# Attention probabilities turned by DMA instead of by TensorE, with scores three heads ahead

## The reference

```python
mod = jax.nn.silu(c) @ w_ada + b_ada
shift, scale, gate = jnp.split(mod, 3, axis=-1)
h = rms_norm(x, g_norm) * (1 + scale) + shift
q_lat, kv_lat, k_rope, z_a, q_b, k_b, v_b, z_b = split(h @ w_in)
# group A: latent attention, 8 heads of 96 (64 + 32 rotary), values of 64
qa = rotate_tail(rms_norm(q_lat, g_qa) @ w_uq);  ka, va = from(rms_norm(kv_lat, g_kva) @ w_ukv, k_rope)
ya = softmax(qa @ ka.T * MLA_SCALE) @ va * silu(z_a)
# group B: 8 query heads of 64 on 2 key heads, norms and 2-D rotary on q and k
yb = softmax(qb @ kb.T * GQA_SCALE) @ vb * silu(z_b)
x = x + gate * (concat(ya, yb) @ w_out)
```

## Time and profile before

| what | value |
|---|---|
| median of 3 runs | 2575.91 us (2571.5 to 2578.02) |
| span of the profiled execution | 2575.7 us |
| its own time, span and what lies around it | not listed apart; the span is within 0.3 us of the median |
| instructions | 44323 |
| TensorE matmuls, weight loads | 16106 each |
| data moved by DMA | 129.42 MB, 50 GB/s over the span |

### The profile page before, as it was taken

One profiled execution on the slowest core, in us unless ns is written; L12 is line 12 of the kernel. 1 busy time (PEld: TensorE's weight loads), 2 busy tenths in 40 slices (PEclk: granted clock), 3 DMA queues, 4 the chain that ended last, 5 costly groups with the idle time before them and its releaser, 6 DMA issues.

```text
span 2575.7 us, 44323 instructions
## 1 busy us (share of the span) xinstructions
PE 2396.8 (93%) x16106; PEld 1409.9 (55%) x16106; DVE 1343.9 (52%) x2390; ACT 974.0 (38%) x2202; POOL 789.5 (31%) x1325
## 2 busy tenths in 40 slices
PE   6689999899999999999989899979899999999997
PEld 1344554455566566666555455545556656656654
DVE  0444444375656565555545444537555556555563
ACT  0223333133444444444422333422344444444442
POOL 0454321274421231232116632237442123123210
PEclk9799999899999999999999999999999999999999
DMA  7621112121000000000242000023000000000001
GB/s 237 222 96 58 54 52 85 58 94 38 9 9 25 16 24 8 24 17 0 73 155 98 9 17 25 33 101 122 9 9 10 33 24 16 24 33 25 0 25 41
DMA packets 63228, 129.42 MB, mean 50 GB/s; under 512 B 6687, under 2 KB 31365, under 8 KB 63125
## 3 DMA queue, kind: packets, MB, share of 16 engines
q1 hardware_dynamic: 63128, 128.09, 14.3%
HBM read 115.44 MB, written 12.63 MB: 50 GB/s over the span
## 4 chain that ended last, share of the span: by engine, by line
PE 75%; DVE 15%; issue 5%; ACT 2%; POOL 1%; DMA 1%; DVEq 0%; SPq 0%; POOLq 0%; ACTq 0%
PE psum L577 58%; PE psum L567 10%; PE psum L770 6%; DVE region L1019 3%; DVE nmax L1002 3%; DVE hT L882 3%; ACT region L1171 1%; DVE region L977 1%; DVE region L1028 0%; DVE region L979 0%; POOL region L1225 0%; PE psum L571 0%; ACT region L1147 0%; DVE KTa L944 0%; DMA Wq<-in_w_ada 0%
## 5 line engine op out<-in xcount | busy, mean ns | idle before, releaser
L1171 ACT ACTIVATE region<-psum 128x512 f16<-128x512 f32 x640 | 353.5, 594 | 769.2 <-PE psum L567 769.2
L577 PE MATMUL psum<-Wq,hT 128*128 128x512 f32 (+1 forms) x1536 | 611.0, 544 | 1.6 <-DVE hT L882 0.6
L1019 DVE TENSOR_TENSOR region<-psum,region 128x512 f16<-128x512 f32 x640 | 415.6, 682 | 293.4 <-ACT region L1171 292.8
L567 PE MATMUL psum<-ident,region 128*128 128x128 f32 (+1 forms) x3208 | 436.9, 277 | 21.5 <-DVE Va L917 10.5
L1002 DVE TENSOR_REDUCE nmax<-psum 128x1 f32<-128x1024 f32 (+1 forms) x384 | 398.6, 1038 | 41.9 <-PE psum L577 41.1
L577 PEld LDWEIGHTS psum<-Wq,hT 128*128 128x128 f32 x1536 | 285.0, 191 | 245.5 <-issue 224.9
L567 PEld LDWEIGHTS psum<-ident,region 128*128 128x128 f32 (+1 forms) x3208 | 356.5, 140 | 105.7 <-issue 78.6
L577 PE MATMUL psum<-Wout,region 128*128 128x512 f32 x768 | 354.5, 607 | 8.5 <-DVE region L987 6.7
L577 PE MATMUL psum<-KTa,region 96*128 96x512 f32 x640 | 311.9, 603 | 18.6 <-DVE region L977 12.9
L1225 POOL TENSOR_TENSOR region<-region,rope_sb 128x64 f32<-128x64 f32 (+3 forms) x384 | 158.3, 434 | 337.7 <-DVE region L973 321.3
L1163 ACT ACTIVATE region<-psum,nmax,unscale 128x1024 f32<-128x1024 f32 (+1 forms) x192 | 204.4, 1064 | 141.7 <-DVE nmax L1005 141.3
(11 more groups left out here) (110 smaller groups left out, 2156.3 us busy)
## 6 DMA issues: line engine op xcount, KB each, us to landing
Wout<-in_w_out SPq DMA_DIRECT2D x8, 2048.0 KB, 11.9
Va<-in_w_ada SPq DMA_DIRECT2D x12, 1024.0 KB, 5.4
Wq<-in_w_in SPq DMA_DIRECT2D x6, 2048.0 KB, 14.3
xn<-x_after_layer SPq DMA_DIRECT2D x24, 512.0 KB, 3.3
Wq<-in_w_ada SPq DMA_DIRECT2D x5, 2048.0 KB, 13.4
xn<-in_x_sample SPq DMA_DIRECT2D x16, 512.0 KB, 3.3
x_after_layer<-region SPq DMA_DIRECT2D x12, 512.0 KB, 2.6
region<-x_after_layer SPq DMA_DIRECT2D x12, 512.0 KB, 3.3
```

The costliest lines, as they stand in the source:

```text
L567: return nc.tensor.transpose(out, in_, ident[0:n, 0:n])
L577: last = nc.tensor.matmul(out, lhsTs[k], rhss[k], start=k == 0, stop=k == n - 1)
L1019: nc.vector.tensor_tensor(PT[:, 1, pt_block(h, S, 4 * c):pt_block(h, S, 4 * c) + 4, :], psum[:, T_BANK + b, :].rearrange("p (c n) -> p c n ...
L1171: nc.scalar.activation(PT[:, 0, pt_block(h, S, 4 * c):pt_block(h, S, 4 * c) + 4, :], psum[:, T_BANK + b, :].rearrange("p (c n) -> p c n", ...
```

## The change

The probabilities are no longer transposed by TensorE. ScalarE makes the exponentials of head h+2 as before in float32 (`probs`), and then copies them in rows into an f16 high part; VectorE subtracts and leaves the f16 low part beside it (`P16`, rows of 2S columns). SyncE turns both parts with one transposing DMA per head from P16 into PT, and `mix` waits for that DMA's semaphore, one per buffer. P16 and PT have 2 buffers with S=1024 and 4 with S=512. Scores run three heads ahead of `mix` instead of two; there are still two score buffers. The high part of a head waits for the DMA of the head that used its buffer; the DMA waits for the low part and for PV of the head that used its PT buffer. VectorE takes the low part behind the next maximum. With S=512 `mix` is no longer a head behind.

As SyncE now waits in these turns, `ada1_load` of the loop and `load_key_weights` of the next stage (with the query weights of layer 1) are issued by ScalarE, the latter in step 5 of the last tile. SyncE's tile loop is written out instead of looped. `Wukv` is loaded after the last PV of a stage (before: after its last transposes). The query weights' semaphore is split in two, c_sb and c_half share the tiles nmax and sums, and the DMA scratch space is set to 256.

The diff, cut to its core:

```diff
+AHEAD_SCORES, AHEAD_PROBS = 3, 2
+P_ROOM = 2 * SMAX
...
+    buffers = [P_ROOM // SEQS[r] for _, r in inst]
...
-        PT = part(region2, SMAX).bitcast(F16).rearrange("p (a c n) -> p a c n", a=2, c=SMAX // P)
+        PT = part(region2, P_ROOM).bitcast(F16)
+        probs = sb("probs", [P, P_ROOM])
+        P16 = sb("P16", [P, 2 * P_ROOM], F16)
...
 @block.sync
             def up_weights(q):
                 if q:
-                    sp.wait_ge(s["tr_ready"], tr_before[q])
+                    sp.wait_ge(s["pv_done"], 16 * before[q])
...
+                def turn(h, i):
+
+                    sp.wait_ge(s["p_low"], heads(b0, i, h))
+                    wait(sp, "pv_done", heads(b0, i, h - buffers[q]))
+                    sp.dma_start_transpose(pt_buf(q, h), parts_buf(q, h)).then_inc(pt_loaded[h % buffers[q]], 16)
+
                 def tile(i, first, last):
                     for h, names in enumerate(completed(first, last, q == 0)):
+                        if h + AHEAD_PROBS < 2 * HEADS or not last:
+                            turn(h + AHEAD_PROBS, i)
                         if last and h == 4 and q + 1 < len(inst):
                             first_rows(q + 1)
-                            if l < DEPTH - 1:
-                                key_weights(q + 1)
...
 @block.tensor
                     wait(pe, "exp_done", heads(b0, i, h - 2))
-                    if h in (0, 1, 4, 8):
+                    if h in (0, 4, 8):
                         pe.wait_ge(s["mm_free"], rounds.now() - later)
...
-                def turn(h, i):
-
-                    pe.wait_ge(s["exp_done"], heads(b0, i, h))
-                    for c in range(nr):
...
+                    wait_pt(pe, q, i, h)
                     for c in range(NT):
-                        if c % 4 == 0:
-                            pe.wait_ge(s["pt_low"], tr_before[q] + nr * heads(0, i, h - 1) + c // 4 + 1)
...
-                        turn(h, i)
...
-                        if h + 2 < 2 * HEADS:
-                            scores(h + 2, i, later)
+                        n = h + AHEAD_SCORES
+                        if n < 2 * HEADS:
+                            scores(n, i, 0 if first and n == 4 else 1)
                         elif not last:
-                            scores(h + 2 - 2 * HEADS, i + 1, later)
+                            scores(n - 2 * HEADS, i + 1, 0)
...
-                        if h or delay == 0 or not first:
-                            mix(h - delay, i)
+                        mix(h, i)
...
 @block.vector
+                def low_part(h, i):
+
+                    dve.wait_ge(s["p_high"], heads(b0, i, h))
+                    parts = parts_buf(q, h)
+                    nc.vector.tensor_tensor(parts[:, S:2 * S], probs_buf(q, h), parts[:, 0:S], ALU.subtract) \
+                        .then_inc(s["p_low"], 1)
...
+                        for name in names[:early]:
+                            side(name, owner(name, i))
+                        next_max(h, i, last)
+                        if h + AHEAD_PROBS < 2 * HEADS or not last:
+                            low_part(h + AHEAD_PROBS, i)
...
 @block.scalar
-                    wait(act, "tr_ready", tr_before[q] + nr * heads(0, i, h - 1 - delay))
+                    wait(act, "p_low", heads(b0, i, h - buffers[q]))
...
+                def high_part(h, i):
+
+                    wait_pt(act, q, i, h - buffers[q])
+                    act.wait_ge(s["exp_done"], heads(b0, i, h))
+                    nc.scalar.activation(parts_buf(q, h)[:, 0:S], probs_buf(q, h), ACT.Copy).then_inc(s["p_high"], 1)
...
+                        next_probabilities(h, i, last)
+                        if last and h == 5 and q + 1 < len(inst) and l < DEPTH - 1:
+                            act.wait_ge(s["scores_ready"], 16 * before[q + 1] - 8)
+                            act.wait_ge(s["mm_ready"], at["z_b"])
+                            load_key_weights(act, q + 1)
...
                         for name in schedule[h - 1] if h else []:
                             query_squares(name, i + 1)
+                            next_ada1(name, i)
```

## The result

The changed kernel takes 2671.26 us (median; 2666.12 to 2673.77), the kernel before beside it on the same chip 2576.11: a ratio of 1.0371, 95% interval 1.0355 to 1.0386. It is slower by 95 us. I had said slower by 37, with 0.48 on slower; the time lies in the range, but the loss is two and a half times the one I worked out.

What follows compares the result with a forecast made beforehand. TensorE was taken to set the pace of the tiles; without transposes, waits for side bank, y and DMA would replace the saving. 2576 + 24 (walk) + 13 (moved steps) = 2613 us, range 2510 to 2900.

Steps and rivals of the forecast that it cites:

- the ceiling: Whole kernel: with the transposes gone from TensorE and nothing in their place, 2576 us would become 2297 us.
- What is removed: TensorE's transposes in all heads: 2560 at 0.109 us, 279 us of work taken off.
- what the transposes covered: Side products' single PSUM bank: waits hidden before now show; middle S=1024 tile waits 9.6 us there, totalling 91.1, not 76.4.
- The low part: VectorE's new 128x1024 subtraction: taken as 1.2 us from operations of similar size; 1.1 gives 15 us less, 1.28 gives 13 more.
- its own table: Whole time by assumed 512 KB landing: -66 us at 3.3, -33 at 4.2, +24 at 5.3, +85 at 6.0, +199 at 7.
- Landing: Transposing DMA per head, issue to landing: 5.3 us for 512 KB, 3.65 us for 256 KB.
- Moved steps: Loads moved to ScalarE's queue: 10 us for seven weight issues ending layer 0, 3 for modulation loads, together +13 us.
- the walk: Hand simulation of each stage's heads, engines in written order, 0.04 us per hand-over; gave +24 us before the moved steps.
- B: Rival: head DMA transposes at the plain rate, landing 3.3 us; -66 us, 2523 us in all; chance 0.24.
- D: Rival: head DMA becomes a stream of small pieces, 26.6 us per 512 KB, some 9000 us in all; chance 0.05.
- C: Rival: two-buffer loop becomes the bound from landings of about 5 us; 2788 us at 7, 2928 at 8; chance 0.17.
- E: Rival: TensorE stays the only bound, side-bank waits hidden by its running ahead; 2297 us and up; chance 0.04.

## Why the prediction was right and wrong

**Right: the ceiling, and the waits behind the transposes.** "What is removed" and "what the transposes covered" hold: 648 instances of the ident products of that group are left, the middle tile's waits stand at the places named (side bank, y, heads 5 and 7), and at full clock the tile takes 90.6 us for the 91.1 forecast. The run with three banks gave 86.0, where 86 to 88 was expected.

**Where it failed, in short.** Four things in the sum were wrong. The low part was priced as if VectorE ran alone (nothing for GpSimd, where quieting a part of GpSimd's work gains 22 us). The moved loads were put at 13 us and measured 31. TensorE's durations were taken at full clock throughout (what that is worth stays open). And the landing was priced too high, which hid a part of the other three: the forecast was too low by 58 us, and by its own table it would have been too low by about 110 with the landing that was measured.

**Landing: priced too high.** The term was 5.3 (3.65) us; it measured 4.3 (3.1). The count of packets was right: of the 33712 packets in the middle tile, 32768 are of 256 B, 2048 a head. They took 22 ns each, not 26 (in the stretch of the earlier trace rows too those of 256 B took 22.6; 26 was the mean with the ones of 512 B): 2048 x 22 ns / 16 = 2.8 us, which leaves 1.5 in place of the fixed 2.0. On the Trainium skill, Advanced Engine Details and Errata, section X-Bar Transpose (TRN2), that transposing DMAs are as fast as regular ones: in landing this run agrees (4.3 beside 4.2 us for xn), but where only transposing DMAs ran in that tile, the engines moved at most 217 GB/s in a fortieth of it and not the 350 to 400 of the page. The other page of the Trainium skill, VectorE: DVE Perf Modes, section The three transpose paths, gives 1309 ns a block; 16 blocks in 4.3 us are 0.27.

**The low part: price right, neighbour missed.** Alone it takes 1.21 to 1.22 us, the 1.2 that I took. But the mean is 1.35 over all of S=1024, and in the first tiles 1.48 and 1.68 with S=1024, and 1.20 and 1.17 for 0.69 with S=512. The step that failed is the choice of the nearest row by size alone. VectorE's subtraction of before read PSUM and SBUF, and no one of the 640 took over 0.69 us, whatever GpSimd did:

```profile
L1019 DVE TENSOR_TENSOR region<-psum,region x640: 671/680/693, 168.8 to 2545.2; 128x512 f16<-128x512 f32 x160
```

The new one reads SBUF twice. I had the rule at hand and did not weigh it: the Trainium skill, SBUF — State Buffer, section SBUF: two separate sides, says that an operation of VectorE with two SBUF inputs and one of GpSimd that reads SBUF exclude each other for the whole instruction. The place at 1994 us agrees: 3.26 us, until GpSimd's 2.34 were over. So do GpSimd's 70 us more of busy time, which I had not looked for. The run with the quiet GpSimd puts the part of the Wout products at some 22 us, their own work included; in the prediction all of it was nothing.

**Moved steps: mis-sized.** I took 10 us for the seven issues and 3 for the modulation loads. The hold was 19.7 us, and moving the weight loads alone gave 31 back. What I left out is that a transposing DMA issued after the loads also waits for them: TensorE stood 10.3 us for one of them in the last tile of layer 0. "A load goes to another queue" was priced by the queue alone, and not by the engines that both queues share.

**The clock: left out.** The sum takes TensorE's durations at full rate, as in the earlier trace rows. In the trace after, TensorE is at the lower of its two levels, 1.2 GHz, for 338 us, in that of before for 105, and outside the key phases and the start for 241 and 17. Laid over the chain that ended last, that is 184 us of TensorE's work at the lower level against 66, an excess of 92 against 33. In time it follows the waits: from 708.6 to 714.8 us TensorE was busy 2.90 of 6.20 us, and in the next 6.20 us the granted clock was 0.72.

```profile
708.60:714.80 6.20, 2.90 (x35) 1.63 (x35) 4.69 (x6) 2.59 (x5) 6.04 (x5) 1.00 0.90 155
714.80:721.00 6.20, 5.97 (x43) 3.33 (x42) 4.40 (x6) 4.06 (x5) 4.88 (x4) 0.72 0.49 93
```

So a wait can cost twice, and a sum of idle time and of durations taken from a stretch without idle time can be too low.

**The account.** With a landing of 4.3 us the forecast's own table gives about -28 us, with the 13 of the moved steps -15, that is 2561 us: faster. The changed kernel is 110 us above that. If the gains add, 18 of the 110 are the loads (31 for 13) and some 22 the low part beside GpSimd's products of Wout. Some 70 us are not shown by a run. By the walk with the measured landings, low parts by tile and SP's issue time they are mostly the clock: it gives +2 us for the +24, and with TensorE's durations divided by the granted clock of each tile +65, near the 59 by which the chain's excess grew. Against so large a price for the clock speak the runs: three banks had 48 us more at half rate and were 76 us faster, the extra work took up to 119 us of half rate away and gave back 14 at most with its own cost in it, and 19 without it by the walk. GpSimd's delay, which the sum does not have, is a rival for the rest: GpSimd came onto the chain in first tiles, and no run took its delay away alone. How the 70 us divide stays open. Open also is the last tile of the first group: without the DMA it falls by 16 us, with late loads by 4; that the modulation loads take the difference was not tried.

**Rivals, and luck.** B's landing of 3.3 us and D's stream of small pieces are out by the rows on the landing. C needs a landing of about 5 us; the median is 4.3, but 27 of the 256 long ones took more, up to 14.9, and ScalarE's high parts waited 149 us for DMAs (116 times): the buffer loop shows in places, though not in the middle tile read above. E is out by the side bank. The forecast's sign was right by luck: the landing that it overpriced stood in for what it had left out.

## What to carry to other kernels

Before work is taken off the engine that sets the pace, list what it hides: a single buffer behind it, a landing, loads on shared DMA engines, and give each its own way out in the same change; here three such ways out turned +95 us into -54. Price a new operation by what its operands share with other engines, not by its size alone. And where the engine will newly wait, take its durations from a stretch in which it waits.

## What the runs showed of the hardware

A subtraction of VectorE with both inputs in SBUF waits whole for a running product of GpSimd: with 1024 columns 1.21 us alone, 3.26 beside a product of 2.34, 3.36 at most; with 512 columns 0.67 to 2.84. With one input in PSUM it took 0.67 to 0.69 for 512 columns throughout. GpSimd stands for VectorE in turn: 1620 ns for 1155 in the mean of one operation, 70 us over the whole. A transposing DMA of 512 KB, f16 rows of 1024 columns in two parts, is 2048 packets of 256 B at some 22 ns, and lands after 4.3 us in the median; 256 KB land after 3.1 and 128 KB after 2.5. Its issue holds SP's queue longer than a plain one:

```profile
L550 SPq DMA_TRANSPOSE region<-P x384: 1231/1798/7327, 165.6 to 2638.2; - x192
```

The least is 1.23 us for 256 KB and 1.55 for 512 KB, the median of all 1.80, a waiting queue included. The 512 KB loads of xn take SP 0.35 us in the median in the same run. And extra TensorE work placed in waits made the changed kernel faster by 14 us, though nobody reads it.
